# A conditioning chunk moved between bodies, its weights in four buffers, and a layer norm split over two engines

## What is computed

```python
def second_block(x, c, w_mod, ...):
    c_act = silu(c)
    for l in range(2):
        mod = c_act @ w_mod[l] + b_mod[l]
        shift, scale, gate = split(mod, 3)
        h = x * (1 + scale) + shift
        y = diff_attention(h, ...) if l == 0 else forgetting_attention(h, ...)   # layer 1: k, v from shared_kv(x, c_act @ w_mod_kv + ...)
        x = layer_norm(ALPHA * x + gate * y, ln_g[l], ln_b[l])
```

## Time and profile before

| | us |
|---|---|
| median of three timed runs (2596.96 to 2603.57) | 2598.83 |
| the profiled execution's own time | 2601.48 |
| span of its profile, first to last instruction | 2599.7 |
| PE busy in the span | 2554.0 |
| DVE busy | 1803.6 |
| ACT busy | 1154.6 |

### The profile page before, as it was taken

How to read it: one execution, slowest core, us unless ns; L and a number is a source line. 1 busy time by engine, 2 the same in 40 slices (tenths; PEclk the granted TensorE clock), 3 DMA queues, 4 the chain that set the end, 5 groups by cost and what they waited for, 6 DMA issues and landing times.

```text
span 2599.7 us, 38429 instructions
## 1 busy us (share of the span) xinstructions
PE 2554.0 (98%) x14550; PEld 2156.5 (83%) x14550; DVE 1803.6 (69%) x2342; ACT 1154.6 (44%) x1475; POOL 0.2 (0%) x4
## 2 busy tenths in 40 slices
PE   8999999999999999999999999999999999999998
PEld 8977878778888888888888888899987778999886
DVE  6897676776667777777776666776786665545756
ACT  5454333445544544444443334333486344334642
POOL 0000000000000000000000000000000000000000
PEclk9999999999999999999999999999999999999999
DMA  6777676776768888888887777888845546675464
GB/s 212 247 236 247 210 249 216 255 255 211 251 227 271 270 276 276 270 272 278 277 276 250 251 253 258 280 275 275 257 138 189 186 159 181 185 230 178 137 215 143
DMA packets 317949, 605.74 MB, mean 233 GB/s; under 512 B 27742, under 2 KB 31844, under 8 KB 316140
## 3 DMA queue, kind: packets, MB, share of 16 engines
q1 hardware_dynamic: 301628, 571.59, 68.3%
q10 hardware_dynamic: 16176, 32.15, 3.6%
HBM read 593.03 MB, written 10.62 MB: 232 GB/s over the span
## 4 chain that ended last, share of the span: by engine, by line
PE 90%; DVE 4%; DMA 2%; ACT 2%; issue 2%; SPq 0%; ACTq 0%; DVEq 0%
PE bank L661 22%; PE bank L663 22%; PE bank L662 22%; PE bank L688 5%; PE bank L686 5%; PE bank L687 5%; DMA gemv_w<-in_w_mod 2%; PE bank L604 2%; PE bank L787 1%; DVE gemv_acc L1927 1%; DVE w_lo L1908 1%; DVE conv_out L2056 1%; ACT w_hi L1281 1%; PE bank L1120 1%; PE bank L813 0%
## 5 line engine op out<-in xcount | busy, mean ns | idle before, releaser
L1908 DVE TENSOR_TENSOR w_lo<-raw,w_hi 128x1024 fp32r<-128x1024 f32 x820 | 1001.7, 1223 | 725.9 <-ACT w_hi L1281 723.9
L1281 ACT CAST w_hi<-raw 128x1024 fp32r<-128x1024 f32 x820 | 859.3, 1049 | 1347.1 <-PE bank L663 1001.7
L661 PE MATMUL bank<-w_hi,u_hi 128*128 128x512 f32 x1216 | 491.9, 404 | 6.3 <-issue 3.8
L663 PE MATMUL bank<-w_hi,u_lo 128*128 128x512 f32 x1216 | 481.2, 396 | 0.0
L662 PE MATMUL bank<-w_lo,u_hi 128*128 128x512 f32 x1216 | 480.9, 395 | 0.0
L1927 DVE SCALAR_TENSOR_TENSOR gemv_acc<-gemv_w,small,gemv_acc 128x512 f32<-128x512 f32 x480 | 357.9, 746 | 23.2 <-DMA gemv_w<-in_w_mod 21.9
L661 PE MATMUL bank<-w_hi,s_hi 128*128 128x512 f32 x744 | 300.9, 404 | 1.3 <-DVE w_lo L1908 1.2
L663 PE MATMUL bank<-w_hi,s_lo 128*128 128x512 f32 x744 | 294.2, 395 | 0.0
L662 PE MATMUL bank<-w_lo,s_hi 128*128 128x512 f32 x744 | 294.2, 395 | 0.0
L688 PE MATMUL bank<-s_hi,w_lo 128*128 128x256 f32 x1024 | 290.1, 283 | 0.0
L687 PE MATMUL bank<-s_lo,w_hi 128*128 128x256 f32 x1024 | 289.5, 283 | 0.0
(11 more groups left out here) (362 smaller groups left out, 2882.6 us busy)
## 6 DMA issues: line engine op xcount, KB each, us to landing
gemv_w<-in_w_mod SPq DMA_DIRECT2D x384, 256.0 KB, 3.2
raw<-in_w_in SPq DMA_DIRECT2D x176, 512.0 KB, 4.5
raw<-in_a_w_in SPq DMA_DIRECT2D x128, 512.0 KB, 4.5
raw<-in_w_ffn_gate SPq DMA_DIRECT2D x88, 512.0 KB, 4.6
raw<-in_w_ffn_up SPq DMA_DIRECT2D x88, 512.0 KB, 4.4
raw<-in_w_ffn_down SPq DMA_DIRECT2D x88, 512.0 KB, 4.3
gemv_w<-in_kv_w_mod SPq DMA_DIRECT2D x128, 256.0 KB, 3.5
raw<-in_kv_w SPq DMA_DIRECT2D x64, 512.0 KB, 3.7
```

What stands on the lines that cost most here:

```text
L661: pe.matmul(o, xh, w_hi[:, s, t], start=(k == 0), stop=False)
L663: ins = pe.matmul(o, xl, w_hi[:, s, t], start=False, stop=(k == 2 * units - 1))
L1281: act.copy(w_hi[:, s], raw[:, s]).then_inc(hi_done, 1)
L1908: dve.tensor_tensor(w_lo[:, s], raw[:, s], w_hi[:, s].bitcast(F32), ALU.subtract).then_inc(lo_done, 1)
```

## The change

Conditioning: `GEMV_RING` = 4 buffers for the weights instead of two, so that SP's load of a step waits for the step four before. `MOD_FROM` leaves out `qkv`'s second body as well as its first, and `MOD_PAUSE` is gone, so that body 6 of `spill` has a chunk. The transpose goes into PSUM bank 7 (`MODB`) instead of `gemv_t`, whose room goes to the buffers; the wait for the stored chunk before moves ahead of it.

Layer norm of layer 0: ACT's dummy root moves to slot 14 of the last body, and the root of the upper half to slot 15, ahead of the last split. DVE makes `SHIFTED` = -mean * root for the upper half. ACT then normalizes the upper half (`upper_normalized`), DVE the lower. PE does 16 matmuls of 512 columns on the old operand `s_hi` into bank 7 before it waits for the normalized blocks; nothing reads their result. The signals `x_mixed` and half of `ln_out` become `x_rows`. Layer 1 gets the earlier dummy root alone.

```diff
 RING = 4
+GEMV_RING = 4
 RMS_EPS = 1e-6
...
         keep = place("keep", [P, KEEP_W], F32)
-        cols = place("cols", [P, 3 * P], F32)
+        cols = place("cols", [P, LN_B + KD], F32)
         modc = place("modc", [P, P], F32)
-        small = place("small", [P, 464], F32)
+        small = place("small", [P, 448], F32)
         stage = place("stage", [P, 2, HALVES, COLS], F32)
         f_first = place("f_first", [P, H3, P], F32, at[0])
-        gemv_w = place("gemv_w", [P, 2, COLS], F32)
+        gemv_w = place("gemv_w", [P, GEMV_RING, COLS], F32)
         gemv_acc = place("gemv_acc", [P, COLS], F32)
-        gemv_t = place("gemv_t", [P, COLS], F32)
         gemv_sums = place("gemv_sums", [P, COLS // SQ], F32)
...
 
+        SHIFTED = 410
         SS, RR, GCOL, BB, EGL, NEGA, ALOG, DTB = 0, 32, 64, 128, 144, 176, 177, 178
         LN_STATS, LN_MOMENTS = 336, 322
         E6, E5, QNS, BFC, MX, SUM, RCP, LAM, RELB, FCOL, CACT = (
-            179, 180, 181, 182, 192, 256, 320, 384, 400, 416, 448)
+            179, 180, 181, 182, 192, 256, 320, 183, 384, 416, 392)
         c_act = small[:, CACT:CACT + KD]
...
         x_in = (sem("x_in0"), sem("x_in1"))
-        gemv_landed = (sem("gemv_landed0"), sem("gemv_landed1"))
+        gemv_landed = [sem(f"gemv_landed{s}") for s in range(GEMV_RING)]
         gemv_cut = sem("gemv_cut")
...
 
-        MOD_FROM, MOD_PAUSE = {"qkv": 1}, {"spill": 6}
+        MOD_FROM = {"qkv": 2}
...
             pr.mods, pr.mod_from = MOD_IN.get(name, 0), MOD_FROM.get(name, 0)
-            pr.mod0, pr.mod_pause = mod0 - pr.mod_from * pr.mods, MOD_PAUSE.get(name, bodies)
+            pr.mod0 = mod0 - pr.mod_from * pr.mods
             pr.cut_ahead0, pr.cut0 = cut0, cut0 + CUT_AHEAD.get(name, 0)
             cut0 = pr.cut0 + bodies * CUT_IN_BODY.get(name, 0)
             unit0, body0, turn0 = unit0 + bodies * units, body0 + bodies, pr.turn0 + bodies * turns
-            mod0 += (bodies - pr.mod_from - (name in MOD_PAUSE)) * pr.mods
+            mod0 += (bodies - pr.mod_from) * pr.mods
         UNITS = unit0
         MOD_CHUNKS = MOD_COLS // COLS
         assert mod0 == MOD_CHUNKS
 
         def without_mod(pr, i):
 
-            return not pr.mods or (isinstance(i, int) and (i < pr.mod_from or i == pr.mod_pause))
-
-        def mod_base(pr, i):
-
-            return pr.mod0 - (pr.mods if isinstance(i, int) and i > pr.mod_pause else 0)
+            return not pr.mods or (isinstance(i, int) and i < pr.mod_from)
...
                     return
-                n = mod_base(pr, i) + m
-                if not (isinstance(i, int) and (n + i * pr.mods) * KD + k < 2):
-
-                    sp.wait_ge(gemv_step, i * (pr.mods * KD) + (n * KD + k - 1))
-                sp.dma_start(gemv_w[:, k % 2], w[k * P:(k + 1) * P, ds(col + m * COLS, COLS)]).then_inc(gemv_landed[k % 2], 16)
+                n = pr.mod0 + m
+                if not (isinstance(i, int) and (n + i * pr.mods) * KD + k < GEMV_RING):
+
+                    sp.wait_ge(gemv_step, i * (pr.mods * KD) + (n * KD + k - (GEMV_RING - 1)))
+                sp.dma_start(gemv_w[:, k % GEMV_RING], w[k * P:(k + 1) * P, ds(col + m * COLS, COLS)]).then_inc(gemv_landed[k % GEMV_RING], 16)
...
             wide_body(pr, 0, w_in[0], 3 * W1, gemv_of(pr, 0, w_mod_2[0], pr.mod0 * COLS), last)
-            with sp.Fori(1, pr.mod_pause) as i:
+            with sp.Fori(1, pr.bodies) as i:
                 wide_body(pr, i, w_in[0], i * 2 * COLS + 3 * W1 + 2 * H1, gemv_of(pr, i, w_mod_2[0], i * COLS + pr.mod0 * COLS),
                           tail_of(pr, gemv_of(pr, i - 1, w_mod_2[0], (i - 1) * COLS + pr.mod0 * COLS)))
-            last = tail_of(pr, gemv_of(pr, pr.mod_pause - 1, w_mod_2[0], (pr.mod_pause - 1 + pr.mod0) * COLS))
-            for i in range(pr.mod_pause, pr.bodies):
-                gemv = gemv_of(pr, i, w_mod_2[0], (mod_base(pr, i) + i) * COLS)
-                wide_body(pr, i, w_in[0], i * 2 * COLS + 3 * W1 + 2 * H1, gemv, last)
-                last = tail_of(pr, gemv)
+            last = tail_of(pr, gemv_of(pr, pr.bodies - 1, w_mod_2[0], (pr.bodies - 1 + pr.mod0) * COLS))
             pr = products["branch"]
...
             def turn_normed(c):
-                pe.wait_ge(signal("ln_out"), HALVES * (c + 1))
+                pe.wait_ge(signal("ln_out"), c + 1)
+                pe.wait_ge(signal("x_rows"), 8 + 1 + c + 1)
 
                 turn_x(products["v3"], c, lambda q: (signal("h_odd"), c) if q else (signal("h_block"), 8 + c))
 
+            for n in range(16):
+                pe.matmul(bank[MODB][:], s_hi[:, n, 0:P], s_hi[:, n // 2 * 2:n // 2 * 2 + 2], start=True, stop=True)
             turn_normed(0)
...
 
+                def first_root():
+                    own.link(act.activation(ln_tmp[layer][:, 0, D - 1:D], sm(E5, 1), ACT.Sqrt, bias=sm(E5, 1)))
+
+                def root_ln(th):
+
+                    act.wait_ge(signal("moments"), HALVES * layer + th + 1)
+                    root(0, sm(LN_MOMENTS + 2 * th + 1), sm(RR + th), 1.0, E5, "root_ln")
+
                 for i in range(pr.bodies):
...
 
-                    body(name, i, nothing, between, finish=(lambda: None) if i == pr.bodies - 1 else None)
-
-                own.link(act.activation(ln_tmp[layer][:, 0, D - 1:D], sm(E5, 1), ACT.Sqrt, bias=sm(E5, 1)))
-                if layer == 0:
-                    act.wait_ge(signal("moments"), HALVES)
-                    root(0, small[:, LN_MOMENTS + 1:LN_MOMENTS + 2 * HALVES:2], sm(RR, HALVES), 1.0, E5, "root_ln")
-                    return
-                for th in range(HALVES):
-                    act.wait_ge(signal("moments"), HALVES + th + 1)
-                    root(0, sm(LN_MOMENTS + 2 * th + 1), sm(RR + th), 1.0, E5, "root_ln")
+                        if layer == 0 and i == pr.bodies - 1 and j == pr.units - 1:
+                            root_ln(0)
+
+                    body(name, i, nothing, between, finish=first_root if i == pr.bodies - 1 else None)
+
+                if layer:
+                    root_ln(0)
+                root_ln(1)
+
+            def upper_normalized(c):
+
+                act.wait_ge(signal("x_rows"), 8 + 1)
+                part = xs[:, 0, c * COLS:(c + 1) * COLS]
+                act.activation(part, part, ACT.Identity, scale=sm(RR), bias=sm(SHIFTED)).then_inc(signal("ln_out"), 1)
...
             layer_tail("o2", "d", 0, forget_weights)
+            upper_normalized(0)
+            upper_normalized(1)
             odd_block(1)
             for q in range(2):
                 v3_operand(q)
             for i in range(2):
                 def between(j, i=i):
+                    if i == 0 and j < 2:
+                        upper_normalized(2 + j)
                     if i == 0 and j < 3:
...
                     return
-                n = mod_base(pr, i) + m
-                c_k, w_k = c_act[:, k:k + 1], gemv_w[:, k % 2]
-                dve.wait_ge(gemv_landed[k % 2], i * (pr.mods * 8 * KD) + (n * 8 * KD + 16 * (k // 2 + 1)))
+                n = pr.mod0 + m
+                c_k, w_k = c_act[:, k:k + 1], gemv_w[:, k % GEMV_RING]
+                dve.wait_ge(gemv_landed[k % GEMV_RING], i * (pr.mods * 4 * KD) + (n * 4 * KD + 16 * (k // GEMV_RING + 1)))
                 if k == 0:
...
                     dve.wait_ge(gemv_step, i * (pr.mods * KD) + (n * KD + KD))
-                    dve.transpose(gemv_t[:], gemv_acc[:]).then_inc(gemv_cut, 1)
-                    dve.wait_ge(gemv_cut, i * (pr.mods * 2) + (2 * n + 1))
                     if not (isinstance(i, int) and i * pr.mods + n == 0):
                         dve.wait_ge(mod_stored, i * (pr.mods * 16) + 16 * n)
-                    dve.tensor_reduce(gemv_sums[:], gemv_t[:].rearrange("p (b c) -> p b c", c=SQ), AX.X, ALU.add).then_inc(
+                    dve.transpose(bank[MODB][:], gemv_acc[:]).then_inc(gemv_cut, 1)
+                    dve.wait_ge(gemv_cut, i * (pr.mods * 2) + (2 * n + 1))
+                    dve.tensor_reduce(gemv_sums[:], bank[MODB][:].rearrange("p (b c) -> p b c", c=SQ), AX.X, ALU.add).then_inc(
                         gemv_cut, 1)
...
                     dve.scalar_tensor_tensor(out=c, in0=c, scalar=ALPHA, in1=stage[:, x, th], op0=ALU.mult,
-                                             op1=ALU.add).then_inc(signal("x_mixed"), 1)
+                                             op1=ALU.add).then_inc(signal("x_rows"), 1)
                 layer, chunk = int(pr is products["o3"]), 2 * i + x
                 for th in ths:
-                    dve.wait_ge(signal("x_mixed"), 8 * layer + 2 * chunk + th + 1)
+                    dve.wait_ge(signal("x_rows"), 13 * layer + 2 * chunk + th + 1)
                     own.inc(dve.bn_stats(sm(LN_STATS + 24 * th + 6 * chunk, 6), xs[:, th, chunk * COLS:(chunk + 1) * COLS]))
...
                         own.inc(centred(0, slice(0, D)))
-                        dve.wait_ge(signal("root_ln"), 2)
+                        dve.wait_ge(signal("root_ln"), 3)
```

(15 more changed lines are left out.)

8 lines of the change are left out of this document (4 added, 4 removed).

## The result

The changed kernel takes 2608.19 us (median of 8 runs, 2606.34 to 2609.96) beside 2599.47 us for the kernel before on the same chip: a ratio of 1.0034, 95% interval 1.0025 to 1.0043. It is slower by 0.34%, about 9 us. The prediction had 2585.0 us and 0.04 for this side. The profiled execution took 2608.25 us, its span is 2606.4.

The account below looks back on a forecast made before the run. PE was taken as the bound, with gains only where it stands still or runs at the lower clock: 8.3 + 3.0 + 2.6 = 13.9 us off the median 2598.83, forecast 2585 us, range 2579 to 2594.

Parts of the forecast that it names:

- at no price: Items priced at nothing: transpose into PSUM and its earlier wait, dummy root, upper-moments wait, `upper_normalized` order, SP's loop.
- A: Second and third `qkv` body and start of `spill`: late `w_lo`, mixer's wait and slow clock shrink; 8.3 us gained.
- B: Body 6 of `spill`: PE's wait for `w_lo` and the slow clock behind it shrink; 3.0 us gained.
- C: Layer norm: PE's idle gap filled, clock kept, blocks ready earlier; 2.6 us gained, bounds 1.0 and 3.8.
- the other nine fit into 18 idle us at no price: Body 6: after seven slots with about 5 us more DVE work, nine slots use DVE's idle time from 562 to 591.
- rival 4: PE's stalls move to the next late piece of the mixer or `v3`; 3 us or less remain, 2596; chance 0.09.
- Rival 2: Mixer's wait stays at the start of `spill`, L2096 as late; 5 us less gain, 2590; chance 0.12.
- Rival 1: Transfers bind in body 6, SP's earlier loads only queue up; B 0 to -3, 2588 to 2591; chance 0.15.
- a sign against itself: Body 6: the prediction is wrong if ACT waits for `raw` there; 8.6 us of such waits before.
- Rival 3: DVE becomes the bound in body 6, 13.4 us exposed: 2601, or 2609 if A's loss stays; chance 0.04.

Follow-up runs that it names:

- 73056: Distance in bytes from `w_hi` to `region`: changed kernel as it is, 2608.19 us; kernel before with `region` 1760 bytes higher, 2612.67 us.
- 71296: Distance in bytes from `w_hi` to `region` in the kernel before; changed kernel with `small` at 440 columns and some small buffers ahead of `raw`: 2591.14 us.
- old order: Changed kernel at 71296 with a chunk in the second `qkv` body again and none in body 6 of `spill`: 2587.97 us, ratio 0.9954.
- the second trace: Kernel before with its whole layout 32 bytes higher: 2600.30 us, ratio 1.0007; its traced execution took 2598.72 us.
- the norm alone: Kernel before, addresses untouched, with only the layer norm part of the change: 2597.01 us, ratio 0.9991.
- 71360: Distance in bytes from `w_hi` to `region`: kernel before with `region` 64 bytes higher, 2567.49 us; changed kernel, 2555.89 us; with the old order, 2555.16 us.

## Why the prediction was wrong

**The missing term.** The prediction summed stalls and let every other matmul cost what it cost before ("there nothing on DVE, ACT or in the DMA queues can be worth anything"). That step failed: the diff's smaller `cols` and `small` and larger `gemv` buffers were not priced at all, not even among the things "at no price". They shift the operands against the weights, and that costs 17.1 us in the changed program (2608.2 - 2591.1), 13.8 in the old one (2612.7 - 2598.9). With 13.9 of gain and 17.1 of loss one gets 3 us slower; the other 6 are stalls, and stretches at the lower clock, that were worth less than thought. By the traces at 73056, the distance of the changed kernel, A is worth 2.8 us, B 1.1 and C 2.7, and 5.0 are left at the last matmul (4.5 by the medians).

**Part A, 8.3 predicted.** 9.0 us by the traces at 71296 beside the trace of before, of which 3.4 up to the first plain matmul (3.3 predicted), the rest the mixer's wait and the clock; beside the trace with everything 32 bytes up 6.6, chiefly since the slow stretch behind the stall is missing there. The 1.6 us for the clock hang on the execution, so that 9.0 stands so near to 8.3 is in part luck. That the buffers are needed was right (0 left with two, 6.9 of the 9.0 with four in the old order). What was wrong was its size at another pace: at 73056 the kernels before and after reach `spill` at 162.88 and 162.91 us and are only 2.8 us apart at the `conv_out` mark. I read it so, which is argued and not tested: a stall caused by a late DVE is counted against PE's pace, and a slower PE waits less.

**Part B, 3.0 predicted, bounds +4.1 and -6.7.** At 71296 2.3 us won by `qk_t`, 2.8 lost behind it up to `mix_hi`: -0.5 (-0.9 beside the second trace). The 1.7 us for the clock are missing in three of the seven traces that have this wait. The step that failed is "the other nine fit into 18 idle us at no price". It is rival 4 at this one place: the stall moved to the next late piece, `probs`, 1.4 us. That DVE is idle for 18 of 29 us does not mean that its chain there has slack. With the pause kept the median is lower (2587.97 beside 2591.14 us), but the runs overlap.

**Part C, 2.6 predicted.** 2.8 us by the trace at its place, no clock loss in the changed kernel (though in two others with the same norm), the first transposes 0.8 us earlier (0.6 predicted). By the medians 0.7 to 1.4 us are left; the prediction had no term for what may happen to the clock some 370 us later.

**Rivals.** Rival 2 (the mixer's wait stays) did not happen: PE waits 0.2 us between 160 and 235 us. Rival 1 (transfers bind) is not shown: ACT's waits for `raw` around body 6 fell from 8.6 to 7.2 us only, which the prediction named as a sign against itself, but PE's waits there end with DVE. Its price for B, 0 to -3 us, is nevertheless what came out at 71296. Rival 3 ended on the right side for the wrong reason: DVE was not the bound in body 6, and its 2601 to 2609 us came from elsewhere.

## What to carry to other kernels

When a change moves or resizes any buffer, compare the pace of untouched matmuls first: the count in a window where PE is 100% busy at the full clock shows in one row what no list of waits can. Fix the distance between streamed and stationary buffers, modulo 256 bytes at least, before comparing schedules, and try it as a knob of its own: here 64 bytes were worth 31 us, four times the whole schedule change. A gain read at a stall is an upper bound; what follows it must be asked what it waits for next.

## What the runs showed of the hardware that was not expected

- With TensorE alone a matmul of 512 columns (weights and columns in float32r) takes 226.7 to 234.1 ns and one of 256 columns 113.3 to 120.0 ns, depending on the distance between weights and columns in SBUF; in the whole kernel, moving both by 32 bytes changes nothing (232.5 and 119.2 ns either way).
- At the distance 71296 one and the same pattern of 256 columns runs at 118.8 ns in `k2` and `q2` and at 120.0 ns in `k3` and `q3` in all traces but one: that of the norm alone has 118.9 there, with the same addresses. At 71360 the two places differ by more, 113.4 and 117.2 ns. So a stream of matmuls can settle into more than one rhythm.
- A wait of PE of 1.9 us is followed by 3.4 us at the lower clock in some kernels and not in others, with the same instructions around it. The same holds of the waits near 176 us (3.9 and 3.5 us) and 548 us (2.4 us in both): in the kernel before each has such a stretch behind it, in the same program with all addresses 32 bytes up neither has. What decides it is open.
